# Stick-breaking attention: a strict mask by matmul, and three places a step for the filling projections

## The reference

```python
def sb_mixer(h, w_in, w_out):
    q, k, v, g = jnp.split(h @ w_in, 4, axis=-1)     # 16 heads of 64
    for i in range(S // BLOCK_Q):
        z = einsum(q_block, k[:, :k_end]) * scale
        strict = (q0 + arange(BLOCK_Q))[:, None] > arange(k_end)[None, :]
        log_beta = log_sigmoid(z)
        log_1m_beta = where(strict, log_sigmoid(-z), 0.0)
        after = cumsum(log_1m_beta, reverse=True) - log_1m_beta
        a = where(strict, exp(log_beta + after), 0.0)
        outs.append(einsum(a, v[:, :k_end]))
    return (o * silu(g)) @ w_out
```

## Time and profile before

| | us |
|---|---|
| median of 3 runs | 3088.73 |
| lowest, highest | 3085.35, 3093.01 |
| span of the profiled execution | 3076.8 |
| TensorE busy in it | 2576.6 (84%) |
| VectorE | 1681.1 (55%) |
| ScalarE | 1241.5 (40%) |
| GpSimd | 607.9 (20%) |

### The profile page before, as it was taken

The page is one execution under the profiler, slowest core; times in us unless marked ns, Lnnn a source line. Parts: engine busy times, 40 slices in busy tenths (PEclk is TensorE's granted clock), DMA queues, the critical chain, the costliest instruction groups (busy, mean ns, idle before and its releaser), DMA issues. The chain is left out here.

```text
span 3076.8 us, 45073 instructions
## 1 busy us (share of the span) xinstructions
PE 2576.6 (84%) x18208; PEld 1488.5 (48%) x18208; DVE 1681.1 (55%) x2370; ACT 1241.5 (40%) x1858; POOL 607.9 (20%) x457
## 2 busy tenths in 40 slices
PE   4899878578989999999996888888888778888876
PEld 1566643235655655555553344444344234655643
DVE  5455453454555555555544667676676434455543
ACT  3322332233433333433433566666666422333221
POOL 2000001210000000000012455555555430000001
PEclk9999999899999999999997899999999888999988
DMA  2111000110010010110102111111111001111001
GB/s 83 35 41 35 30 28 28 55 29 14 29 31 22 32 39 18 35 38 16 44 15 57 33 43 34 48 43 48 28 47 37 14 29 35 35 35 35 29 28 69
DMA packets 42162, 109.55 MB, mean 36 GB/s; under 512 B 6979, under 2 KB 11331, under 8 KB 41957
## 3 DMA queue, kind: packets, MB, share of 16 engines
q1 hardware_dynamic: 41956, 106.68, 11.6%
HBM read 85.68 MB, written 4.19 MB: 29 GB/s over the span
## 5 line engine op out<-in xcount | busy, mean ns | idle before, releaser
L219 PE MATMUL psum<-h_hi,gla_w_hi 128*128 128x512 f16 (+1 forms) x544 | 215.9, 397 | 93.1 <-issue 48.1
L1416 ACT ACTIVATE mla_prob<-psum,mla_neg_top 128x128 f32<-128x128 f32 (+7 forms) x128 | 94.8, 740 | 369.5 <-DVE mla_neg_top L1320 344.8
L918 POOL TENSOR_TENSOR sb_al<-sb_zc,sb_ah 128x256 f16<-128x256 f32 (+2 forms) x96 | 171.8, 1790 | 220.6 <-ACT sb_ah L873 220.6
L220 PE MATMUL psum<-h_lo,gla_w_hi 128*128 128x512 f16 (+1 forms) x544 | 215.1, 395 | 0.0
L221 PE MATMUL psum<-h_hi,gla_w_lo 128*128 128x512 f16 (+1 forms) x544 | 215.0, 395 | 0.0
L1338 DVE TENSOR_TENSOR mla_pt_lo<-psum,mla_pt_hi 128x128 f16<-128x128 f32 (+7 forms) x128 | 97.0, 758 | 203.1 <-ACT mla_pt_hi L1424 203.1
L907 POOL TENSOR_TENSOR sb_zc<-sb_zc,sb_el 128x256 f32<-128x256 f32 (+2 forms) x96 | 174.6, 1818 | 137.5 <-ACT sb_el L850 137.3
L1213 PE MATMUL psum<-mla_diag,mla_prob 128*128 128x128 f32 x1152 | 160.0, 285 | 48.4 <-DVE mla_diag L1332 48.3
L1480 POOL TENSOR_TENSOR mla_y_lo<-mla_yt,mla_y_hi 128x512 f16<-128x512 f32 x32 | 37.0, 1157 | 770.9 <-ACT mla_y_hi L1432 770.9
L235 PE MATMUL psum<-gla_w_hi,h_hi 128*128 128x128 f16 x1024 | 173.8, 219 | 10.9 <-issue 10.9
L1213 PEld LDWEIGHTS psum<-mla_diag,mla_prob 128*128 128x128 f32 x1152 | 144.4, 196 | 70.0 <-DVE mla_diag L1332 66.1
(11 more groups left out here) (320 smaller groups left out, 7285.7 us busy)
## 6 DMA issues: line engine op xcount, KB each, us to landing
sb_wf<-in_sb_in SPq DMA_DIRECT2D x32, 512.0 KB, 3.6
gla_wf<-in_gla_v SPq DMA_DIRECT2D x16, 512.0 KB, 3.5
gla_wf<-in_gla_g SPq DMA_DIRECT2D x16, 512.0 KB, 3.5
gla_wf<-in_gla_out SPq DMA_DIRECT2D x16, 512.0 KB, 3.5
mla_wf<-in_mla_gate SPq DMA_DIRECT2D x16, 512.0 KB, 3.6
mla_wf<-in_mla_out SPq DMA_DIRECT2D x16, 512.0 KB, 3.6
xT<-in_x_T SPq DMA_DIRECT2D x8, 512.0 KB, 6.4
gla_wf<-in_gla_q SPq DMA_DIRECT2D x8, 512.0 KB, 3.5
```

What stands on the lines that cost most here:

```text
L219: pe.matmul(out, wh[:, w], act_hi[:, k, tok], start=(i == 0), stop=False)
L220: pe.matmul(out, wh[:, w], act_lo[:, k, tok], start=False, stop=False)
L918: pool.tensor_tensor(self.al[s % 2][:, :, off:HALF], self.zc[s % 3][:, :, off:HALF], self.ah[s % 2][:, :, off:HALF], ALU.subtract).then_in ...
L1416: act.activation(self.prob[t % 2][:, 0:w], self.pair(t)[:, 0:w], ACT.Exp, bias=self.neg_top[:, k], scale=self.SCALE, accum_out=self.total[ ...
```

## The change

The mask is now added to the scores. Two constants are made: `mask_w`, 32768 on the diagonal and 0 elsewhere, and `mask_k`, -60000 where the key is not earlier than the query. Their product, added by one matmul of 128 columns for each head into the diagonal part of the scores, makes a masked score about -2e9. Then ln(1 + exp) is 0, `Lf` is 0, and the weight is exp of a very negative number, 0. The multiplication on VectorE and the select on GpSimd fall away, and their waits with them.

And a third place for the fillings is put in each step, between `z` and `t`.

```diff
@@ attention
-            out = [("z", s + 1)] if more else []
+            out = [("z", s + 1), ("gap", 1)] if more else []
             out.append(("t", s))
@@ pe
                 pe.matmul(out, k, self.q_hh[:, p % 2, h, q], start=True, stop=False)
+                if j >= 4 * g:
+                    pe.matmul(L.bank(h)[:, off:off + P], self.mask_w[:], self.mask_k[:], start=False, stop=False)
                 mm = pe.matmul(out, k, self.q_ll[:, p % 2, h, q], start=False, stop=True)
@@ dve, item l
-            dve.wait_ge(self.L_ready, s + 1)
-            if j >= 4 * g:
-                d = self.Lf[:, :, off:off + P]
-                dve.tensor_tensor(d, d, self.mask[:], ALU.mult).then_inc(self.Lm_ready, 1)
             dve.wait_ge(self.Lh_ready, s + 1)
@@ dve, item t
-            self.wait_lb(dve, s)
+            dve.wait_ge(self.lb_ready, s + 1)
@@ act, item l
-            if j >= 4 * g:
-                act.wait_ge(self.Lm_ready, self.diag_count(s))
@@ pool, start
-            pool.memset(self.mask[:], 1.0).then_inc(self.consts, 1)
-            pool.wait_ge(self.consts, 3)
+            pool.memset(self.mask_w[:], self.MASK_GAIN).then_inc(self.consts, 1)
+            pool.memset(self.mask_k[:], self.MASK).then_inc(self.consts, 1)
+            pool.wait_ge(self.consts, 4)
...
@@ pool, item l
-            if j >= 4 * g:
-                pool.wait_ge(self.lb_ready, s + 1)
-                pool.affine_select(out=lb[:, :, off:off + P], in_=lb[:, :, off:off + P], compare_op=ALU.is_gt,
...
```

More of the change, by code:

```diff
@@ L512 @@
     SHIFT = 3
+    MASK = -60000.0
+    MASK_GAIN = 32768.0
     STEPS = [(g, j) for g in range(2) for j in range(4 * g + 3, -1, -1)]
@@ L536, in __init__ @@
             self.not_later = sb("not_later_key", [P, P], F16)
-            self.mask = sb("strict_mask", [P, 2, P], F32)
+            self.mask_w, self.mask_k = sb("mask_w", [P, P], F16), sb("mask_k", [P, P], F16)
             self.gain = sb("gain", [P, KD], F32)
@@ L551, in __init__ @@
             self.L_ready = sem("L_ready")
-            self.Lm_ready = sem("Lm_ready")
             self.Lh_ready = sem("Lh_ready")
@@ L555, in __init__ @@
             self.lb_ready = sem("lb_ready")
-            self.lbm_ready = sem("lbm_ready")
             self.s_ready = sem("s_ready")
@@ L648, in pe @@
         if kind == "start":
-            pe.wait_ge(self.consts, 4)
+            pe.wait_ge(self.consts, 6)
             self.norm.pe(pe)
@@ L785, in dve @@
                 self.dve_y(dve, s)
[L787 to L793, removed]
-        if j >= 4 * g:
-            eng.wait_ge(self.lbm_ready, self.diag_count(s))
-        eng.wait_ge(self.lb_ready, s + 1)
     def scale_of(self, name):
@@ L858, in act @@
             s, = a
-            p, _, _, g, j, off = self.where(s)
+            off = self.where(s)[-1]
             act.wait_ge(self.L_ready, s + 1)
-            if j >= 4 * g:
-                act.wait_ge(self.Lm_ready, self.diag_count(s))
             if s >= 2:
@@ L894, in pool @@
                                base=0, pattern=[[1, P]], channel_multiplier=-1)
-            pool.affine_select(out=self.mask[:], in_=self.mask[:], compare_op=ALU.is_gt, fill=0.0, base=0,
-                               pattern=[[0, 2], [1, P]], channel_multiplier=-1).then_inc(self.consts, 1)
+            pool.affine_select(out=self.mask_w[:], in_=self.mask_w[:], compare_op=ALU.is_equal, fill=0.0, base=0,
+                               pattern=[[-1, P]], channel_multiplier=1).then_inc(self.consts, 1)
+            pool.affine_select(out=self.mask_k[:], in_=self.mask_k[:], compare_op=ALU.is_ge, fill=0.0, base=0,
+                               pattern=[[-1, P]], channel_multiplier=1).then_inc(self.consts, 1)
             self.norm.pool(pool)
@@ L903, in pool @@
             s, = a
-            _, _, _, g, j, off = self.where(s)
+            off = self.where(s)[-1]
             lb = self.zc[s % 3]
@@ L908, in pool @@
                                ALU.subtract).then_inc(self.lb_ready, 1)
-            if j >= 4 * g:
-                pool.wait_ge(self.lb_ready, s + 1)
-                pool.affine_select(out=lb[:, :, off:off + P], in_=lb[:, :, off:off + P], compare_op=ALU.is_gt,
-                                   fill=-1e30, base=0, pattern=[[0, 2], [1, P]],
-                                   channel_multiplier=-1).then_inc(self.lbm_ready, 1)
         elif kind == "a":
```

## The result

| | before | after |
|---|---|---|
| median us, runs on one chip | 3087.45 | 3196.36 |
| lowest, highest | 3085.35, 3093.01 | 3192.04, 3199.56 |
| span of the profiled execution | 3076.8 | 3196.0 |

The ratio is 1.0347 [1.0335, 1.0359]: the change costs 108.9 us. The sign and the range were right, the forecast of 3215 was 18.6 too high. Medians and ratios are of fast executions: one of the four of e8_late_halves, 3170.25 us at a granted clock of 0.844, was a slow one and is left out.

A forecast was written before the change was run, and what follows sets the result against it. A VectorE-ScalarE loop bounds the kernel. Seven woven pairs at +18.7 add 131, the last pair returns 3, matmuls cost 2: +130 on 3076.8, plus 11.9, gives 3219, lowered for slack to 3215 us; range 3138 to 3245.

The forecast's parts named there:

- The loop that bounds the kernel, and the mask: Attention part: a VectorE-ScalarE loop sets the pace; removing the mask gains 63 us, its added matmuls cost 2.
- The order in the split step: Full-width weight-split step: `w_lo` could start at +4.44, subtraction at 6.82, `Lf` 7.96, next `zc` 13.9 at low clock.
- The hold: Full-width split steps: `w_lo` stands until GpSimd's L907 is over, 1.2 us each, some 20 us in the sum.
- TensorE comes onto the path: Matmul `c` waits for the subtraction; this becomes TensorE's largest wait in the part, about 20 us a pair.
- The clock: TensorE's idles before `c` halve the clock in full-width split and first-unit steps, adding 1.95 us each; part's clock below 0.85.
- Around the span: The median of the runs stands 11.9 us above the profiled span, added to the forecast.
- The variant in which the clock falls only in the split steps: Rival: no clock fall in first-unit steps, 14.8 us a pair, 3190; chance 0.18.
- Full clock: Rival: the new TensorE idles do not bring the clock down, +8.6 us a pair, 3147; chance 0.20.
- No hold: Rival: `w_lo` is not held by GpSimd, 20 us less, 3127 at the least; chance 0.05.
- Covered: Rival: the gap before `Lf` takes in the VectorE halves, leaving the mask's gain alone, 3028; chance 0.07.
- It cancels: Rival: the place costs no more than 8 us a pair and the mask pays for it, 3080 to 3098; chance 0.05.

The follow-up runs named there:

- e8_late_halves: Kernel after with ScalarE's halves back behind `l` and VectorE's halves of w, q, k, v after the next `zc`: 3007.84 us.
- e1_mask_only: Kernel after without the third place, so the mask by matmul alone: 3025.45 us.
- e2_place_only: Kernel before with the third place added and the old mask kept: 3211.85 us.
- e4_split_first: Kernel after, with GpSimd's `zc - el` (L896) waiting for `w_lo` in the weight-split steps: 3154.36 us.
- e7_kept_busy: Kernel after with zero matmuls filling TensorE's idle ahead of `c` in steps 1, 5, 7, 8, 10, 11: 3157.82 us.
- e11_first_busy: Kernel after with GpSimd's L896 waiting for `w_lo` and fewer zero matmuls than e7_kept_busy: 3132.77 us.
- e9_late_units: As e8_late_halves, but only VectorE's halves of q, k, v units come late; weight splits stay behind `l`: 3002.47 us.
- e10_units_busy: e5_split_back with zero matmuls ahead of `c` in steps 5, 8 and 11: 3077.68 us.
- e5_split_back: Kernel after with only the weight splits' ScalarE, VectorE and SyncE work moved back behind `l`: 3090.18 us.

## Why the prediction was right

**The loop that bounds the kernel, and the mask.** Right. The working gave 63 us less 2 for the matmuls; e1_mask_only measured 61. That it would be worth only 15 beside the place (after against e2_place_only) was not worked out as a number of its own, but the steps' lengths had it in: step 7 was put at 13.15 with the mask's gain "in", and TensorE's chain ending it.

**The order in the split step.** Right to 0.15 us: `w_lo` at +4.37 (forecast 4.44), its end 1.08 after GpSimd's, the subtraction at +6.82 (6.82), `Lf` at +7.95 (7.96), the next `zc` at +13.75 (13.9).

**The hold.** The trace shows `w_lo` beside L896, which the trace of before did not: 2.52 us, ending 1.08 behind it. The Trainium skill, "SBUF — State Buffer", section "Who interferes with whom", has it so: the second of the two stands until the first is through. The trace agrees, and e4_split_first shows the other case, 1.22 us. Without the hold the prediction gave some 20 us less; at the full clock it was 25 (e7_kept_busy against e11_first_busy), and 42 where the falls of the clock changed with it (e4_split_first). The term itself was right, 1.31 us a full-width split step for 1.2; it left out the 0.6 of step 1.

**TensorE comes onto the path.** Right: its wait ahead of `c` is 145.4 us, about 21 a pair (forecast 20), and `zc` now waits for scores.

**The clock.** This is the step that failed in size. The prediction added 1.95 us to every split step and every first-unit step of width, "each such idle adds 1.95". In step 11 the clock fell in one pair of seven. Step 11 of after, in a pair where it stayed, and the first matmul of `c` in the first pair, where it fell:

```profile
2127.18 0.69 DVE L457 SCALAR_TENSOR_TENSOR sb_v_lo<-psum,sb_v_hi 128x512 f16<-128x512 f32 x1 [2.70 <-ACT sb_v_hi L450]
2127.79 1.21 DVE L779 TENSOR_TENSOR sb_zc<-sb_zc,psum 128x1024 f32<-128x1024 f32 x1
...
2129.06 0.39 PE L704 MATMUL psum<-sb_Lh,sb_not_later_key 128*128 128x512 f16 x1 [2.30 <-DVE sb_zc L779]
...
1803.27 0.61 PE L704 MATMUL psum<-sb_Lh,sb_not_later_key 128*128 128x512 f16 x1 [2.29 <-DVE sb_zc L779]
```

The idle is 2.30 us, near the forecast of about 2.6, and in six pairs all of `c` runs at full speed; the step takes 9.43, forecast 11.2. In the first pair it takes 11.08, as forecast. In step 8 the clock fell in 5 of 7 pairs. The same instructions run in both cases. What differs ahead of them is how long the low clock lasted in step 7, but that is not the reason by itself: in e2_place_only the clock of step 7 is 0.74, and step 8 stays at 1.00. Windows of steps 7 and 8, first of a pair where it did not fall in step 8, then of one where it did:

```profile
2079.54:2092.22 12.68, 7.00 (x32) 2.92 (x31) 6.96 (x6) 5.70 (x6) 4.95 (x3) 0.87 0.49 124
2092.22:2101.98 9.76, 7.38 (x37) 3.04 (x36) 5.41 (x6) 5.67 (x6) 3.17 (x3) 1.00 0.00 2
...
2185.45:2199.67 14.22, 8.53 (x32) 3.24 (x31) 6.96 (x6) 5.70 (x6) 5.02 (x3) 0.76 0.43 112
2199.67:2211.06 11.39, 9.01 (x37) 3.40 (x36) 5.40 (x5) 5.67 (x6) 4.57 (x2) 0.85 0.00 1
```

The clock of the part should have fallen below 0.85; it fell to 0.89. What a fall costs, read against e7_kept_busy: 1.5 to 1.6 us in steps 1, 8 and 10, and 1.3 or 2.8 in step 7. The size of 1.95 was fair, the number of falls too high. Single steps missed in both directions, so the pair's total is nearer than its parts: in four pairs step 7 was 1.1 longer than forecast, while step 11 was 1.8 shorter. And it had no term for the idle of 2.65 us ahead of the scores in step 4, behind which the clock is 0.78 over step 5. In the sum: a woven pair grew by 13.7 to 17.0, not 18.7, seven of them by 109.6, not 131; the last pair brought back 0.9, not 3.

**Around the span.** The prediction read the 11.9 us between the median and the profiled span as work around it. The profiled execution of after took 3197.74, 1.7 more than its span. The rest, some 10 us, was that the profiled execution of before was a quick one: with the same 1.7 it comes to 3078.5, under every timed run of that kernel (lowest 3082.7). The first `zc` stands at 1696.19 there and at 1700.66 to 1708.93 in all the others, the layers ahead being the same. It did no harm here: the medians grew by just what the part grew by, so adding the part's growth to the median was the right sum, for another reason than was given.

**The rivals.** The variant in which the clock falls only in the split steps, 3190 with a chance of 0.18, came nearer to the 3196.4 than the forecast did: it fell in steps 1, 7 and 10 of every woven pair but for step 1 of the first, in step 8 in five pairs of seven, in step 11 in one. *Full clock* (3147) is nearly e7_kept_busy, 3157.8; the kernel after stands between it and the forecast. *No hold* is e4_split_first. *Covered* was excluded by the order, as said, and e9_late_units shows what it takes. *It cancels* would have needed a place at 8 us a pair; it costs 25.

## What to carry to other kernels

A place in a common list of work is a place on every engine's queue. Work that one engine can do while it waits drags its halves on the other engines along, and a half put where its input is not ready holds all that is queued behind it: give each engine its own place for it, behind the main work of the step, or in a gap where its input has long been there and which is longer than it, with its time counted as it is beside what the other engines do there (0.68 us into 1.09 paid; a split of 1.22, held to 2.18 and 2.63, did not). When two changes come as one, time each alone: here a gain of 61 us lay under a loss of three times that.

## What the runs showed of the hardware

Whether the clock falls after an idle of about 2 us can't be read from the idle. After 2.38 us ahead of `c` in step 8 it stayed at 1.00 in two pairs and fell in five, with the same instructions; after the same 2.38 in e4_split_first it stayed in all seven. After 2.30 us in step 11 it stayed in six and fell in one; in e10_units_busy it fell after 1.99 us in six of seven, with zeros just ahead. In the earlier trace rows 1.99 did not bring it down and 2.25 did. After 2.80 us in step 1 of e4_split_first it never fell, after 3.40 in step 1 of after always, and after 3.78 in e5_split_back in five of seven. After 4.38 us and more (up to 6.16, in steps 7, 8 and 10 of five kernels) it was low in every pair with filling. A forecast should give idles of 2 to 4 us a share of the cost, not all of it.

Here is step 8 of a pair where it fell, after 2.38 us; compare 0.38 for each of these matmuls where it did not:

```profile
2205.47 0.39 PE L704 MATMUL psum<-sb_Lh,sb_not_later_key 128*128 128x512 f16 x1 [2.38 <-DVE sb_zc L779]
...
2205.91 0.48 PE L704 MATMUL psum<-sb_Lh,sb_not_later_key 128*128 128x512 f16 x1
...
2206.19 0.63 PE L704 MATMUL psum<-sb_Ll,sb_not_later_key 128*128 128x512 f16 x1
```

Keeping TensorE busy with matmuls on zeros buys the clock back, 39 us here for 80 us of added busy time, but the order that made the idle cost more: up to 116 us, the unfilled low stretch over steps 4 and 5 among them.

A held operation ends 1.08 us behind the GpSimd one that holds it, for 1024 elements: `w_lo` beside L896 in steps 7 and 10 of after, and beside L935 in steps 8 and 11 of e8_late_halves.
